# GpSimd subtracts the mean from tiles 4 to 7 in the layer norms over 1024 features

## The chip, the cores and the metric

The kernel runs on one core of a Trainium2 chip. The core has TensorE (PE in the profile), VectorE (DVE), ScalarE (ACT), GpSimd (POOL) and a sync engine (SP) that issues DMAs. Time is device microseconds (us) of one execution.

## The reference, cut to what matters

Two model blocks run one after the other on 512 positions of 1024 features, in float32. The first block has six layer norms over the 1024 features, three in each of its two layers:

```python
def layer_norm(x, g, b):
    mu = jnp.mean(xf, axis=-1, keepdims=True)
    var = jnp.mean(jnp.square(xf - mu), axis=-1, keepdims=True)
    y = (xf - mu) * lax.rsqrt(var + LN_EPS) * g + b
...
for l in range(DEPTH):                       # DEPTH is 2
    ...                                      # a mixer gives y
    x = layer_norm(ALPHA * x + y, ln_mix_g[l], ln_mix_b[l])
    y = memory_cross_attention(x, mem_n, ...)
    x = layer_norm(ALPHA * x + y, ln_xa_g[l], ln_xa_b[l])
    y = swiglu_ffn(x, ffn_wg[l], ffn_wu[l], ffn_wd[l])
    x = layer_norm(ALPHA * x + y, ln_ffn_g[l], ln_ffn_b[l])
```

Two more layer norms (of the memory, and of 512 convolution channels) and the RMS norms of the second block are computed by the same engines and are not changed.

## The kernel before, in words

**Layout.** The activations `xs` lie in on-chip memory as 8 tiles (k = 0 to 7) of 128 features by 512 positions. Each float32 product is made of three matmuls: every operand is split in a high part (`xh`, `w_hi`) and the rest (`xl`, `w_lo`), and `mm3` (L630) adds high by high, high by rest and rest by high. ScalarE makes the high parts, VectorE the rests. Weights come in 205 units of 128x2048, double buffered: SP loads `w_raw`, ScalarE copies it to `w_hi` (`split_hi`, L1139), VectorE subtracts to get `w_lo` (`split_lo`, L1627), and TensorE may begin a unit only when its `w_lo` is there.

**Order.** There is no scheduler. Each engine has its own hand-written list, and the engines meet at semaphores. An engine that waits holds all that stands behind it in its list.

**A layer norm.** The names are mixn0, xan0, ffnn0, mixn1, xan1, ffnn1 in order of time. TensorE sums `xs` and its squares over the features by matmuls with ones, so each sum is already broadcast to all 128 partitions. ScalarE copies the mean out of the bank (L1170, it signals `mean_ready`) and squares it into `rstd` (L1171). Then VectorE runs `normalise` (L1704):

1. `centre(0)`: subtract the mean from tile 0 (L1710);
2. `variance`: mean of squares minus squared mean (L1689, one input a bank, one on chip), then clamp and add epsilon (L1691). ScalarE takes Ln and Exp of it (L1161, L1163) and signals `rstd_ready`;
3. `centre(1)` to `centre(3)`;
4. in the four norms with a filler (mixn0, xan0, ffnn0, mixn1), `w_lo` of a filler unit;
5. for k = 0 to 7: multiply tile k by `rstd` (L1724), then `centre(k + 4)` while k + 4 is below 8, then `then(k - 1)`. With a filler, `w_lo` of one more unit stands in front of k = 2;
6. `then(7)` and `w_lo` of the next unit.

`then(k)` makes the rest `xl` of tile k (L1635), after ScalarE has applied gain and bias to the tile (L1198) and made its high part `xh` (L1152). In ffnn0 `then` is `pool`, the causal window means of the next mixer (L2118, L2110, L2124), which run on VectorE for a pair of tiles at every odd k. In ffnn1 it also collects sums of squares, and ScalarE makes a square for each tile too (L1158).

**Fillers.** In the four norms with a filler, TensorE computes two units of keys or values of the memory while the statistics are made. In xan1 and ffnn1 there is nothing to put there, and TensorE waits for tile 0.

**GpSimd** only clears a few tiles and issues DMAs: constants at the start, then, at L606 to L610, it waits until TensorE has used the unit ahead of glr (near 1421 us), clears part of `wgk` and loads `wgk` and two constants for the second block.

Of the kernel before, what the change touches and what calls it, by code (L numbers as in the profile page):

```python
# [25 lines left out]
ALU = mybir.AluOpType  # L26
# [4 lines left out]
KT = D // P  # L31
# [88 lines left out]
def plan_banks():  # L120
# [24 lines left out]
    def pairs(stage, n):  # L145
        for j in range(n):
            pair(stage, j)

    def norm(name, has_mean=True):
        if has_mean:  # L150
            fill((name, "mean"), 6)
        fill((name, "sq"), 7)
# [15 lines left out]
    def linear_attention(name, filler):  # L168
        for h in range(HEADS):
            fill((name, "scores", h), 4)  # L170
            fill((name, "kend", h), 5)
            if filler:
                pair(*filler[2 * h])
            if h:
                fill((name, "ssq", h - 1), 6 + h % 2)
            fill((name, "o", h, 0), 6 + h % 2)
            fill((name, "ds", h, 0), 4)
            fill((name, "ds", h, 1), 5)
            if filler:
                pair(*filler[2 * h + 1])  # L180
            fill((name, "ds", h, 2), 4)
            fill((name, "ds", h, 3), 5)
        fill((name, "ssq", HEADS - 1), 6)
# [62 lines left out]
    pairs("g", 2), pairs("a1", 1), pairs("q", 2), pairs("v", 2)  # L246
    linear_attention("hg", HG_FILLER)
    norm("cvn")
# [44 lines left out]

FILLER = {"mixn0": "mk1a", "xan0": "mk1b", "ffnn0": "mv1a", "mixn1": "mv1b"}
SUMMED = 2
HG_FILLER = [("mk0", j) for j in range(4)] + [("mv0", j) for j in range(4)]
SWA_ITEMS = 16
plan_banks()
# [30 lines left out]
class Seen:  # L329
# [18 lines left out]
    "sq_ready",  # L348
    "sq_used",
    "mean_ready",  # L350
    "var_ready",
    "rstd_ready",
    "zn_ready",
# [21 lines left out]
def build(nc, x, mem, params, consts, table, w_gk2, sinks, w, out):  # L375
    scratch = nc.dram_tensor("rel_scratch", [16, 384], F32, kind="Internal").ap()
    with ExitStack() as ctx:
        def sb(stack, name, shape, dt=F32):
            return stack.enter_context(nc.sbuf_tensor(name, shape, dt))

        def new_sem(name):
            return ctx.enter_context(nc.semaphore(name))

        sem = {n: new_sem(n) for n in SIGNALS}
# [40 lines left out]
        xs = sb(ctx, "xs", [P, KT, T])  # L425
# [8 lines left out]
        mean = sb(ctx, "mean", [P, T])  # L434
# [79 lines left out]
        def bank(key):  # L514
            return banks[FILL[key][0]]
# [9 lines left out]
        def wait_free(eng, key, i=None):  # L525

            b, n, per = FILL[key][:3]
            if n:
                eng.wait_ge(bank_free[b], at(i, per, n))

        def wait_drained(eng, key, i=None):

            b, n, per = FILL[key][:3]
            eng.wait_ge(bank_free[b], at(i, per, n + 1))
# [4 lines left out]
        def col(name, k=0):  # L539
            c = COL[name] + k  # L540
            return prm[:, c:c + 1]
# [40 lines left out]
        @block.gpsimd  # L582
        def _(pool):
            def const(dst, name, signal, rows=P):
                c = CCOL[name]
                pool.dma_start(dst, consts[0:rows, c:c + dict(CONSTS)[name]]).then_inc(signal, 16)


            pool.memset(ones[:, :], 1.0).then_inc(ones_ready, 1)
            pool.wait_ge(ones_ready, 1)  # L590
            pool.memset(cu[:, :, 0:TAPS - 1], 0.0).then_inc(ones_ready, 1)
            pool.dma_start(prm[:, :], params).then_inc(prm_loaded, 16)
            pool.wait_ge(x_loaded[3], 16)
            pool.dma_start(mk[:, :, :], mem).then_inc(mem_loaded, 16)
            const(sum_q[:, :], "scan32", scan32_loaded)
            const(hmask[:, :], "mask32", hmask_loaded)
            const(ident[:, :], "ident", ident_loaded)
            const(invpos[:, :], "invpos", invpos_loaded)
            pool.dma_start(skb[:, :], sinks.partition_broadcast(P)).then_inc(sinks_loaded, 16)
            pool.wait_ge(ones_ready, 2)  # L600
            pool.memset(tab[32:33, :], NEG).then_inc(ones_ready, 1)
            pool.dma_start(tab[0:32, :], table[0:32, :]).then_inc(table_loaded, 16)

            pool.wait_ge(unit_used, UNITS["glr"])
            pool.wait_ge(ones_ready, 3)
            pool.memset(wgk[96:128, :], 0.0).then_inc(ones_ready, 1)  # L606
            pool.wait_ge(ones_ready, 4)
            pool.dma_start(wgk[112:128, :], w_gk2).then_inc(wgk_loaded, 16)
            const(gmask[:, :], "mask64", gmask_loaded)
            const(scan64[:, :], "scan64", scan64_loaded)  # L610

            pool.wait_ge(unit_used, UNITS["mlp0"])
            const(kk[0:33, 0, 0:384], "onehot", onehot_loaded, 33)
            const(flip[:, :], "flip", flip_loaded)
            wait_drained(pool, ("vec", 0))
            pool.dma_start(scratch, vt[0:16, 0:384]).then_inc(vec_stored, 16)
            pool.wait_ge(vec_stored, 16)

            hankel = bass.AP(tensor=scratch.tensor, offset=0, ap=[[1, P], [384, 16], [1, 2 * P]])
            pool.dma_start(sf[:, :].rearrange("p (h k) -> p h k", h=16), hankel).then_inc(hankel_loaded, 16)  # L620
# [3 lines left out]
        def _(pe):  # L624
            seen = Seen(pe, sem)

            def mm(dst, a, b, start, stop):
                return pe.matmul(dst, a, b, start=start, stop=stop)  # L628
# [51 lines left out]
            def layer_norm_sums(name, x_at, wait_tile, tiles=KT, all_tiles=False):  # L680
# [3 lines left out]
                if all_tiles:  # L684
                    wait_free(pe, mean_)
                    for k in range(tiles - SUMMED):
                        wait_tile(k)
                        mm(bank(mean_)[:, :], ones[:, :], x_at(k), k == 0, False)
                seen.next("sq_used", tiles - SUMMED - 1)
                if not all_tiles:  # L690
# [3 lines left out]
                mm(bank(sq_)[:, :], ones[:, :], sum_q[:, :], True, False)  # L694
                for k in range(tiles - SUMMED, tiles):
                    wait_tile(k)
# [4 lines left out]
            def squares_of_last(key, tiles=KT):  # L701
                seen.skip("sq_ready", tiles - SUMMED)
                for k in range(tiles - SUMMED, tiles):
                    seen.next("sq_ready")
                    last = mm(bank(key)[:, :], ones[:, :], sq[:, k % 2, :], False, k == tiles - 1)
                full(last, key)
# [7 lines left out]
            def rms_norm_sums(name, token_major=False):  # L714

                key, tok = (name, "sq"), (name, "tok")
                seen.next("sq_used", KT - SUMMED - 1)
                wait_free(pe, key)
# [247 lines left out]
            wait_drained(pe, ("v", 1, 1))  # L966
            linear_attention("hg", 32, hq, hk, hs, henb, kend_hg, lambda t, c, n: hv[:, t, c:c + n], 1, HG_FILLER)

# [156 lines left out]
        def _(act):  # L1125
# [309 lines left out]
            def values_out(j):  # L1435
                for m in range(2):
                    key = ("v", j, m)
                    drain(key, hv[:, 2 * m:2 * m + 2, j * 256:(j + 1) * 256], bank(key)[:, :].rearrange("p (t n) -> p t n", t=2))
# [3 lines left out]
            split_hi(UNITS["v"] + 2)  # L1442
            linear_attention("hg", 32, hb, heb, henb, kend_hg, 1.0, 1, lambda h, d: hq[:, h, :], HG_FILLER,
                             lambda: values_out(1))
# [164 lines left out]
        def _(dve):  # L1609
            seen = Seen(dve, sem)  # L1610
            steps = Tally(dve, dve_steps)
# [92 lines left out]
            def normalise(name, n, x_at, tiles, then, unit=None, stage=None):  # L1704


                centred = {}

                def centre(k):
                    centred[k] = steps.step(dve.tensor_tensor(x_at(k), x_at(k), mean[:, :], ALU.subtract))  # L1710

                seen.next("mean_ready")
                centre(0)
                variance(name, n)
                for k in range(1, 4):
                    centre(k)
                if stage:
                    split_lo(unit + 1)
                seen.next("rstd_ready")
                for k in range(tiles):  # L1720
                    if stage and k == 2:
                        split_lo(unit + 2)
                    steps.wait(centred[k])
                    give(dve.tensor_tensor(x_at(k), x_at(k), rstd[:, :], ALU.mult), "zn_ready")  # L1724
                    if k + 4 < tiles:
                        centre(k + 4)
                    if k:
                        then(k - 1)
                then(tiles - 1)
                split_lo(unit + 3 if stage else unit + 1)  # L1730
# [341 lines left out]
            def clear_kpad():  # L2072
# [4 lines left out]
            linear_attention("hg", 32, hq, hk, hb, heb, henb, hmask[:, :], hs, 1, lambda h, d: hq[:, h, :],  # L2077
                             lambda h, d: hg[:, h, :], lambda h, d: col("hg_g", h), HG_FILLER, clear_kpad)
            own("conv_ready")
# [292 lines left out]
```

## Time and profile before

| | |
|---|---|
| median of 3 runs | 2647.96 us (2647.86 to 2650.87) |
| the profiled execution's own time | 2647.57 us |
| its span in the trace | 2645.8 us |
| TensorE busy | 2503.9 us, 95% |
| VectorE busy | 1506.0 us, 57% |
| ScalarE busy | 881.4 us, 33% |
| GpSimd busy | 9.9 us |
| mean granted TensorE clock | 0.976 of 2.4 GHz |

The profiled execution's time is 1.8 us longer than its span and 0.4 us below the median. Busy shares are means over the whole program. In a norm they say little: there TensorE waits and VectorE and ScalarE hand the tiles to each other.

### The profile page before, as it was taken

What the parts mean: (1) busy time and instruction counts of PE and PEld (TensorE: products, weight loads), DVE (VectorE), ACT (ScalarE), POOL (GpSimd) and SP (SyncE); (2) the same over time, 40 slices, a digit from 0 to 9 for tenths busy, and PEclk for the clock granted to TensorE, in tenths of its full rate; (3) what the DMA queues carried; (4) which work ended last, traced back from release to release, by engine and by line L of the source; (5) the groups of instructions that cost most, each with busy time, mean ns of one, the idle gap of its engine ahead of it and who ended that gap; (6) DMA issues with size and microseconds to landing.
All of it is one profiled execution on the core that took longest, in us unless ns stands there. A gap on an engine that the chain in (4) does not pass through costs nothing.

```text
span 2645.8 us, 29702 instructions
## 1 busy us (share of the span) xinstructions
PE 2503.9 (95%) x11776; PEld 2046.3 (77%) x11776; DVE 1506.0 (57%) x2043; ACT 881.4 (33%) x1184; POOL 9.9 (0%) x23
## 2 busy tenths in 40 slices
PE   8998999999999798999997998999999977999998
PEld 7887777788887576888885797788888766788886
DVE  6887544544446835544447436566666467566666
ACT  3434443422223633322224334322222445322222
POOL 0000000000000000000000000000000000000000
PEclk9999999999999899999998999999999998999999
DMA  5222221222222111222221220232222200222221
GB/s 184 80 80 80 80 80 64 96 95 95 95 97 94 64 64 64 93 98 95 95 95 56 93 96 17 92 117 95 95 95 95 80 32 17 84 101 100 96 95 64
DMA packets 32815, 225.56 MB, mean 85 GB/s; under 512 B 3765, under 2 KB 3813, under 8 KB 6368
## 3 DMA queue, kind: packets, MB, share of 16 engines
q1 hardware_dynamic: 31536, 220.21, 24.3%
q0 software_dynamic: 1200, 4.23, 0.4%
q8 instruction: 57, 0.93, 0.1%
q14 instruction: 22, 0.18, 0.0%
HBM read 222.30 MB, written 2.12 MB: 85 GB/s over the span
## 4 chain that ended last, share of the span: by engine, by line
PE 83%; DVE 10%; ACT 5%; issue 1%; DMA 0%; DVEq 0%; SPq 0%; ACTq 0%
PE bank L628 82%; DVE w_lo L1627 2%; ACT w_hi L1139 1%; ACT xs L1198 1%; ACT xh L1152 1%; DVE cacc L1815 1%; DVE xs L1710 1%; DVE xl L1635 0%; DVE mh L2240 0%; DVE xs L1679 0%; DVE rmax L2259 0%; DVE xs L1724 0%; DVE gs L1866 0%; ACT mh L1590 0%; DVE mh L2256 0%
## 5 line engine op out<-in xcount | busy, mean ns | idle before, releaser
L628 PE MATMUL bank<-xh,w_hi 128*128 128x512 f32 x2040 | 816.0, 400 | 62.9 <-DVE xl L1635 27.3
L628 PE MATMUL bank<-xl,w_hi 128*128 128x512 f32 x2040 | 805.7, 395 | 0.0
L628 PE MATMUL bank<-xh,w_lo 128*128 128x512 f32 x2040 | 804.8, 395 | 0.0
L1627 DVE TENSOR_TENSOR w_lo<-w_raw,w_hi 128x2048 fp32r<-128x2048 f32 x205 | 469.7, 2291 | 407.6 <-ACT w_hi L1139 407.1
L1139 ACT ACTIVATE w_hi<-w_raw 128x2048 fp32r<-128x2048 f32 x205 | 391.3, 1909 | 398.6 <-PE bank L628 398.5
L628 PEld LDWEIGHTS bank<-xh,w_hi 128*128 128x128 f32 x2040 | 389.6, 191 | 165.6 <-issue 29.8
L628 PEld LDWEIGHTS bank<-xh,w_lo 128*128 128x128 f32 x2040 | 389.9, 191 | 83.4
L628 PEld LDWEIGHTS bank<-xl,w_hi 128*128 128x128 f32 x2040 | 390.4, 191 | 81.3 <-issue 2.2
L1679 DVE TENSOR_TENSOR xs<-xs,bank 128x512 f32<-128x512 f32 x448 | 294.4, 684 | 116.2 <-PE bank L628 115.1
L628 PE MATMUL bank<-mhh,w_lo 128*128 128x512 f32 x512 | 199.2, 389 | 0.0
L628 PE MATMUL bank<-mhh,w_hi 128*128 128x512 f32 x512 | 199.2, 389 | 0.0
L628 PE MATMUL bank<-mhl,w_hi 128*128 128x512 f32 x512 | 199.2, 389 | 0.0
L1767 DVE TENSOR_TENSOR mh<-bank,rstd 128x512 f32<-128x512 f32 x64 | 43.9, 692 | 178.6 <-PE bank L628 178.6
L1261 ACT ACTIVATE mhh<-mh 128x512 fp32r<-128x512 f32 x64 | 39.5, 633 | 317.3 <-DVE mh L1772 317.3
L628 PE MATMUL bank<-fhh,w_hi 128*128 128x512 f32 x352 | 136.9, 389 | 0.0
L628 PE MATMUL bank<-fhl,w_hi 128*128 128x512 f32 x352 | 136.9, 389 | 0.0
L628 PE MATMUL bank<-fhh,w_lo 128*128 128x512 f32 x352 | 136.9, 389 | 0.0
L1158 ACT ACTIVATE sq<-xs 128x512 f32<-128x512 f32 x88 | 54.6, 630 | 192.1 <-DVE xs L1679 70.7
L628 PEld LDWEIGHTS bank<-mhh,w_lo 128*128 128x128 f32 x512 | 96.1, 188 | 20.1
L628 PEld LDWEIGHTS bank<-mhl,w_hi 128*128 128x128 f32 x512 | 96.1, 188 | 20.0
L628 PEld LDWEIGHTS bank<-mhh,w_hi 128*128 128x128 f32 x512 | 96.1, 188 | 19.9
L1765 DVE TENSOR_TENSOR fh<-sil,bank 128x512 f32<-128x512 f32 x44 | 30.0, 688 | 116.6 <-PE bank L628 109.5
(284 smaller groups left out, 2626.5 us busy)
## 6 DMA issues: line engine op xcount, KB each, us to landing
w_raw<-weights_in SPq DMA_DIRECT2D x205, 1024.0 KB, 5.0
xs<-x_in SPq DMA_DIRECT2D x4, 512.0 KB, 8.1
sf<-rel_scratch POOLq DMA_DIRECT2D x1, 2048.0 KB, 11.8
y_out<-xs SPq DMA_DIRECT2D x8, 256.0 KB, 2.0
w_raw<-weights_in SPq DMA_DIRECT2D x2, 512.0 KB, 6.8
mk<-mem_in POOLq DMA_DIRECT2D x1, 1024.0 KB, 7.2
sum_q<-consts_in POOLq DMA_DIRECT2D x1, 256.0 KB, 7.3
scan<-consts_in POOLq DMA_DIRECT2D x1, 256.0 KB, 2.8
```

Source lines behind the costliest of these rows:

```text
L628: return pe.matmul(dst, a, b, start=start, stop=stop)
L1139: act.activation(w_hi[:, c % 2, :], w_raw[:, c % 2, :], ACT.Copy).then_inc(w_hi_ready, 1)
L1152: give(act.activation((xh if dst is None else dst)[:, k, :], src, ACT.Copy, **kw), "x_hi")
L1158: give(act.activation(sq[:, k % 2, :], src, ACT.Square), "sq_ready")
L1198: give(act.activation(xs[:, k, :], xs[:, k, :], ACT.Identity, scale=col(f"{param}_g{l}", k), bias=col(f"{param}_b{l}", k)), "xn_ready")
L1261: give(act.activation(hh[:, chunk % 2, m, :], src, ACT.Copy), "hh_ready")
L1627: dve.tensor_tensor(w_lo[:, c % 2, :], w_raw[:, c % 2, :], w_hi[:, c % 2, :].bitcast(F32), ALU.subtract)\
L1679: free(dve.tensor_tensor(xs[:, k, :], xs[:, k, :], bank(key)[:, :], ALU.add), key)
L1710: centred[k] = steps.step(dve.tensor_tensor(x_at(k), x_at(k), mean[:, :], ALU.subtract))
L1765: free(dve.tensor_tensor(hid[:, m, :], sil[:, m, :], bank(key)[:, :], ALU.mult), key)
L1767: free(dve.tensor_tensor(hid[:, chunk % 2, m, :], bank(key)[:, :], rstd[:, :], ALU.mult), key)
L1815: ins = dve.scalar_tensor_tensor(a, u, wj, a, ALU.mult, ALU.add)
```

## The change

GpSimd subtracts the mean from tiles 4 to 7 in the six norms over 1024 features: it waits for `mean_ready`, does four subtractions and signals `late_centred` after each. VectorE subtracts it from tiles 0 to 3 only, and waits for `late_centred` ahead of the product with `rstd` of tiles 4 to 7. GpSimd's clear of `wgk` and the DMAs behind it now stand behind all 24 subtractions. The index in `NORMS_WITH_MEAN` plus one is the value of `mean_ready` that belongs to a norm.

```diff
+EARLY = 4
+NORMS_WITH_MEAN = ["memn", "cvn", "mixn0", "xan0", "ffnn0", "mixn1", "xan1", "ffnn1"]
...
+            def centre_late_tiles(norm):
+                pool.wait_ge(sem["mean_ready"], NORMS_WITH_MEAN.index(norm) + 1)
+                for k in range(EARLY, KT):
+                    pool.tensor_tensor(xs[:, k, :], xs[:, k, :], mean[:, :], ALU.subtract).then_inc(sem["late_centred"], 1)
+
+            for norm in NORMS_WITH_MEAN[2:]:
+                centre_late_tiles(norm)
+
             pool.wait_ge(unit_used, UNITS["glr"])
             pool.wait_ge(ones_ready, 3)
+            pool.wait_ge(sem["late_centred"], (KT - EARLY) * len(NORMS_WITH_MEAN[2:]))
             pool.memset(wgk[96:128, :], 0.0).then_inc(ones_ready, 1)
...
-                for k in range(1, 4):
+                for k in range(1, EARLY):
                     centre(k)
...
-                    steps.wait(centred[k])
+                    if k < EARLY:
+                        steps.wait(centred[k])
+                    else:
+                        seen.next("late_centred")
                     give(dve.tensor_tensor(x_at(k), x_at(k), rstd[:, :], ALU.mult), "zn_ready")
-                    if k + 4 < tiles:
-                        centre(k + 4)
```

VectorE's list in mixn0, before, from the clamp of the variance on. `xs<-xs,mean` is a subtraction of the mean, `xs<-xs,rstd` the product with the reciprocal root, `xl` the rest of a tile, `w_lo` the rest of a weight unit:

```order
L1691 TENSOR_SCALAR rstd<-rstd 128x512 [waits bank_free7]
L1710 TENSOR_TENSOR xs<-xs,mean 128x512 x3
L1627 TENSOR_TENSOR w_lo<-w_raw,w_hi 128x2048 [waits w_hi_ready]
L1724 TENSOR_TENSOR xs<-xs,rstd 128x512 [waits dve_steps,rstd_ready]
L1710 TENSOR_TENSOR xs<-xs,mean 128x512
L1724 TENSOR_TENSOR xs<-xs,rstd 128x512 [waits dve_steps]
L1710 TENSOR_TENSOR xs<-xs,mean 128x512
L1635 TENSOR_TENSOR xl<-xs,xh 128x512 [waits x_hi]
L1627 TENSOR_TENSOR w_lo<-w_raw,w_hi 128x2048 [waits w_hi_ready]
L1724 TENSOR_TENSOR xs<-xs,rstd 128x512 [waits dve_steps]
L1710 TENSOR_TENSOR xs<-xs,mean 128x512
```

The same place with the change (its lines are numbered 12 to 15 higher):

```order
L1703 TENSOR_SCALAR rstd<-rstd 128x512 [waits bank_free7]
L1722 TENSOR_TENSOR xs<-xs,mean 128x512 x3
L1639 TENSOR_TENSOR w_lo<-w_raw,w_hi 128x2048 [waits w_hi_ready]
L1739 TENSOR_TENSOR xs<-xs,rstd 128x512 [waits dve_steps,rstd_ready]
L1739 TENSOR_TENSOR xs<-xs,rstd 128x512 [waits dve_steps]
L1647 TENSOR_TENSOR xl<-xs,xh 128x512 [waits x_hi]
L1639 TENSOR_TENSOR w_lo<-w_raw,w_hi 128x2048 [waits w_hi_ready]
L1739 TENSOR_TENSOR xs<-xs,rstd 128x512 [waits dve_steps]
```

Nothing ahead of the first product with `rstd` has moved. Behind it the four single subtractions are gone.

GpSimd's list with the change, from its last DMA of the start to `wgk`; before, the clear of `wgk` followed that DMA directly. The pair of rows that begins with a wait for `mean_ready` comes six times in all, one pair for each norm, and stands once here:

```order
L605 DMA tab<-table_in 32x16
L610 ISA
L610 TENSOR_TENSOR xs<-xs,mean 128x512 [waits mean_ready]
L610 TENSOR_TENSOR xs<-xs,mean 128x512 x3
...
L618 MEMSET wgk 32x512 [waits late_centred,ones_ready,unit_used]
L620 DMA wgk<-w_gk_in 16x512 [waits ones_ready]
```

What moved: 24 subtractions of 128x512 onto GpSimd, and the clear of `wgk` and the DMAs behind the last of them.

## Rows read from the trace of the kernel before

**Rows 1.** The page: engines' busy time, and the shares of the chain that ended last.

```profile
PE 2503.9 (95%) x11776; PEld 2046.3 (77%) x11776; DVE 1506.0 (57%) x2043; ACT 881.4 (33%) x1184; POOL 9.9 (0%) x23
...
PE 83%; DVE 10%; ACT 5%; issue 1%; DMA 0%; DVEq 0%; SPq 0%; ACTq 0%
```

**Rows 2.** L1710 alone: count, ns min/median/max, first and last start.

```profile
L1710 DVE TENSOR_TENSOR xs<-xs,mean x48: 682/685/693, 320.2 to 1438.2; 128x512 f32<-128x512 f32 x48
```

**Rows 3.** Timeline of DVE in mixn0: start us, us, engine, line, what, [idle before, releaser].

```profile
320.15 0.69 DVE L1710 TENSOR_TENSOR xs<-xs,mean 128x512 f32<-128x512 f32 x1 [4.40 <-ACT mean L1170]
320.76 0.68 DVE L1689 SCALAR_TENSOR_TENSOR rstd<-bank,rstd 128x512 f32<-128x512 f32 x1
321.48 0.43 DVE L1691 TENSOR_SCALAR rstd<-rstd 128x512 f32<-128x512 f32 x1
321.82 1.89 DVE L1710 TENSOR_TENSOR xs<-xs,mean 128x512 f32<-128x512 f32 x3
323.63 2.28 DVE L1627 TENSOR_TENSOR w_lo<-w_raw,w_hi 128x2048 fp32r<-128x2048 f32 x1
325.83 0.69 DVE L1724 TENSOR_TENSOR xs<-xs,rstd 128x512 f32<-128x512 f32 x1
...
330.42 2.29 DVE L1627 TENSOR_TENSOR w_lo<-w_raw,w_hi 128x2048 fp32r<-128x2048 f32 x1 [1.49 <-ACT w_hi L1139]
...
333.23 0.68 DVE L1710 TENSOR_TENSOR xs<-xs,mean 128x512 f32<-128x512 f32 x1
...
334.43 0.68 DVE L1724 TENSOR_TENSOR xs<-xs,rstd 128x512 f32<-128x512 f32 x1
...
336.24 0.69 DVE L1724 TENSOR_TENSOR xs<-xs,rstd 128x512 f32<-128x512 f32 x1
```

**Rows 4.** Timeline of ACT in mixn0, tile 0 and tile 3, same columns.

```profile
326.55 0.82 ACT L1198 ACTIVATE xs<-xs,prm 128x512 f32<-128x512 f32 x1 [3.31 <-DVE xs L1724]
...
335.15 0.82 ACT L1198 ACTIVATE xs<-xs,prm 128x512 f32<-128x512 f32 x1 [0.33 <-DVE xs L1724]
```

**Rows 5.** End of mixn0 in the chain that ended last: start us, us, what.

```profile
344.59 0.69 DVE xl L1635
345.28 2.21 DVE w_lo L1627
...
347.54 12.51 PE bank L628 x54
```

**Rows 6.** Timeline of ACT in xan1, tiles 2 and 3.

```profile
1058.88 0.81 ACT L1198 ACTIVATE xs<-xs,prm 128x512 f32<-128x512 f32 x1 [0.17 <-DVE xs L1724]
...
1060.69 0.81 ACT L1198 ACTIVATE xs<-xs,prm 128x512 f32<-128x512 f32 x1 [0.32 <-DVE xs L1724]
```

**Rows 7.** Timeline of DVE in xan1 (first row) and in ffnn0 (the others).

```profile
1052.28 0.69 DVE L1689 SCALAR_TENSOR_TENSOR rstd<-bank,rstd 128x512 f32<-128x512 f32 x1 [0.39 <-PE bank L628]
...
861.44 0.69 DVE L1710 TENSOR_TENSOR xs<-xs,mean 128x512 f32<-128x512 f32 x1
862.23 1.23 DVE L2118 TENSOR_TENSOR pb<-pa 128x1024 f32<-128x1024 f32 x1
```

**Rows 8.** Timeline of POOL: clears of 1 and of 512 columns.

```profile
0.26 0.10 POOL L2362 MEMSET const-float32-0.0<- 128x1 f32 x1 [0.26 <-issue]
...
1421.05 0.52 POOL L606 MEMSET wgk<- 32x512 f32 x1 [1404.19 <-PE bank L628]
```

**Rows 9.** Timeline of DVE beside that last clear.

```profile
1421.14 0.69 DVE L1649 TENSOR_TENSOR sum_q<-sum_q,sq 128x512 f32<-128x512 f32 x1
```

**Rows 10.** Groups of DVE by shape: busy us, mean ns, idle before. One input, on chip or bank.

```profile
L1738 DVE TENSOR_SCALAR xs<-xs 128x512 f32<-128x512 f32 x16 | 5.5, 421 | 0.0
...
L1695 DVE TENSOR_SCALAR rstd<-bank 128x512 f32<-128x512 f32 x13 | 8.9, 687 | 21.7 <-PE bank L628 21.7
```

**Rows 11.** The tile wgk: its first and last matmul start.

```profile
L628 PE MATMUL bank<-mh,wgk x8: 587/587/692, 1483.7 to 1486.8; 32*128 32x512 f32 x8
```

**Rows 12.** Stretches of xan1: busy us by engine, then PEclk, DMA share, GB/s.

```profile
1060.00:1065.00 5.00, 5.00 (x15) 3.90 (x14) 3.67 (x7) 4.61 (x6) 0.00 (x0) 0.58 0.00 0
```

More of the change, by code:

```diff
@@ L350 @@
     "mean_ready",
+    "late_centred",
     "var_ready",
```

## The prediction, made before the changed kernel ran

> **What bounds the kernel now.** I read the page first: TensorE is busy 95% of the span, and 83% of the chain that ended last is TensorE [rows 1]. GpSimd is nearly empty. So a change to VectorE's work counts only where TensorE waits for VectorE, and the six norms are such places. I then read them engine by engine in the timelines. In mixn0 TensorE's next unit starts at 347.54, right behind a `w_lo` that follows the rest of tile 7 at 344.59 [rows 5]. That rest waits for ScalarE, which works through tiles 3 to 7 without a pause for VectorE once tile 3's gain step has begun at 335.15 [rows 4]. So **the second half of a norm goes at ScalarE's pace**, and its end is set by when tile 3's product is there. The first half is VectorE's: from 320.15 to the first product at 325.83 its instructions stand end to end [rows 3], and ScalarE has sat idle for 3.31 us when tile 0 arrives [rows 4]. Whatever delays VectorE in those 5.7 us moves the whole norm. The four subtractions that the change takes from VectorE all stand behind them.
>
> **Part 1: what VectorE loses.** Each subtraction takes 0.685 us by itself [rows 2], but instructions overlap a little: starts lie 0.60 us apart, as 333.23 to the next one shows with two instructions up to 334.43 [rows 3]. Four of them in six norms are 24 x 0.60 = 14.4 us of VectorE. Nearly all of that is off the path, because ScalarE sets the pace. Norm by norm:
> - mixn0, and xan0 and mixn1, whose rows repeat it: tile 3's product starts at 334.43, behind the subtraction at 333.23 [rows 3]. Without it the product is 0.60 us earlier, but ScalarE was idle for only 0.33 us there [rows 4]. Gain 0.3 us each, 0.9 in all. The two subtractions ahead of the `w_lo` at 330.42 give nothing: that one waits for ScalarE, with 1.49 us idle in front of it [rows 3].
> - xan1: ScalarE idles 0.17 and 0.32 us ahead of tiles 2 and 3 [rows 6]. Gain 0.5 us.
> - ffnn0: the subtraction at 861.44 stands directly ahead of the pooling at 862.23 [rows 7], for which everything waits. Gain 0.6 us. The three others there lie in waits.
> - ffnn1: ScalarE has a third step for each tile and is never idle behind tile 0. Gain 0.
>
> Sum: **-2.0 us** (0.9 + 0.5 + 0.6). It is the whole gain that the change can bring.
>
> **Part 2: how long a GpSimd subtraction takes.** No row shows GpSimd reading anything. The nearest are its clears: 0.10 us for one column and 0.52 us for 512 [rows 8], so 0.42 us for one stream of 512 columns. A subtraction has two streams in and one out. If all overlap, it takes 0.52 us, the lower bound. If the three follow one another, it takes 0.10 + 3 x 0.42 = 1.36 us, the upper one. Two inputs in turn with the output beside them would be 0.94. I take 1.15, the middle of the last two, since an engine that needs 0.8 ns for a column that it only writes is unlikely to be as fast when it has to fetch two.
>
> The Trainium skill ("GPSIMD Engine Reference", section 3.1) gives 4497 ns for a float32 `tensor_tensor` of 2048 columns. A quarter of that, 1.12 us, is an estimate from that page, and by it the sum of part 3 would be lower by some 0.7 us. No run here shows it yet.
>
> **Part 3: what these subtractions do to VectorE.** GpSimd is released by the same signal as VectorE's `centre(0)`, so its 4 x 1.15 = 4.6 us fall exactly on the stretch from 320.15 to 325.83. The question is whether both engines can read on-chip tiles at once. The one overlap in the trace is harmless: VectorE's addition at 1421.14 keeps its 0.69 us beside the clear at 1421.05 [rows 8, 9]. But a clear reads nothing. Another pair of rows speaks for a limit on reading: with one on-chip input VectorE needs 0.42 us for 512 columns, and 0.69 when that input is a bank [rows 10]. So it has two ways into on-chip memory and uses both for one tile if it can. A subtraction with two on-chip inputs takes 0.69 us and needs both, and a third reader must share with one of them.
>
> The ends are: no loss (0 us) and full exclusion. For exclusion, I let the engines alternate, each instruction in full:
> - Norms with a filler (four): GpSimd's first subtraction runs behind `centre(0)`, beside the variance step, which takes its second input from a bank; there 0.7 us are free (320.76 to 321.48 [rows 3]). The other three go between the clamp, the three subtractions and the 2.28 us `w_lo`, all ahead of the first product. Delay 4 x 1.15 - 0.7 = 3.9 us each, 15.6 in all.
> - xan1 and ffnn1: VectorE also waits 0.39 us for a bank ahead of the variance [rows 7], so the first subtraction is free. Delay 3 x 1.15 = 3.45 us each, 6.9 in all.
>
> That makes **+22.5 us**. By the bounds of part 2 it would be 4 x 1.38 + 2 x 1.56 = 8.6 (0.52 us a subtraction) or 4 x 4.74 + 2 x 4.08 = 27.1 (1.36 us). A delay of the first product reaches the end of the norm in full. ScalarE waits for it, `w_hi` of the next unit stands behind tile 0 on ScalarE, and the following `w_lo` waits for that. I choose exclusion over no loss because rows 10 are nearer to the case (they are about reading) than rows 9.
>
> What the Trainium skill says on this ("SBUF — State Buffer", section "Who interferes with whom") is sharper: GpSimd's only read port is VectorE's second one, the pair is an exclusive lock for a whole instruction, and a VectorE instruction with two on-chip inputs contends with a GpSimd one that reads. By that rule the sum is the one with exclusion, by rows 9 alone it would be that of part 1. The rule speaks against the change.
>
> **Part 4: the rest.** The wait for tile 4 stands ahead of the product at 336.24, which is 16 us behind the mean [rows 3]. Four GpSimd subtractions need less than 6, so it costs nothing; even in xan1, where tile 4 is due some 10 us after the mean, each could take 2.4 us. With that cover gone, every us of lateness would reach the end. Ahead of its first subtraction GpSimd's list has one instruction of its own kind, `ISA`; it stands in front of the wait, some 300 us early. The clear of `wgk` and three DMAs move from 1421 to behind ffnn1, near 1435, but the first matmul that reads `wgk` starts at 1483.7 [rows 11]: cost 0, with some 45 us to spare. The added wait on `late_centred` at the clear is met by then. PE and ScalarE issue the same lists as before.
>
> **The clock.** When TensorE waits longer, its clock can fall: in xan1 it waited for tile 0, and the stretch behind had a granted clock of 0.58 of 2.4 GHz, so mostly the lower level, 1.2 GHz [rows 12]. There TensorE still kept up with ScalarE. In the norms with a filler the added wait falls between two filler units, where a few us at the lower level would cost 1 to 2 us each. I put 0 in the sum and up to 7 us in the range.
>
> **The sum.** 2647.57 (the profiled execution) + 22.5 - 2.0 = 2668.1. The execution lies 0.4 us below the median of the runs, which is less than what I can resolve. I predict **2668 us**, 0.8% slower.
>
> **Rivals.**
> 1. *Both engines read at once.* It happens ahead of the first product, in all six norms. GpSimd's work is then wholly hidden: 2647.6 - 2.0 = 2645.6, no measurable change. For it: rows 9. Against it: rows 10. It decides on the stretch that one GpSimd subtraction puts on VectorE: below 2.0 / 24 = 0.08 us the kernel gains, and up to 0.3 us each (7.3 / 24) it stays within 0.2%.
> 2. *VectorE goes first.* If VectorE, whose instructions overlap at their ends, holds on to the memory while it has work, GpSimd only gets its turn in VectorE's pauses: beside the variance (1.15 against 0.7 free, +0.45), then in the pause of 1.49 us at 328.9 and in others like it. Price 0.5 to 1.2 us a norm, some +5, less 2.0: near 2650.5. For it: in VectorE's timeline an instruction starts before the one ahead has ended. Against it: a request of GpSimd's that waits is older than VectorE's next one.
> 3. *They share instead of excluding.* Each slows the other in part, say half of part 3: +11 - 2 = 2656.6.
> 4. *The change doesn't do what it says*: an index of `mean_ready` off by one would let GpSimd start in an earlier norm. The sequence memn, cvn, mixn0 and so on agrees with the eight ScalarE copies of a mean, so I give it nothing.
> 5. *A gain above 0.2%* would need 5 us, and part 1 has only 2.0 on the path. It would take a shift of fillers or clock that no row shows.
>
> **How the numbers follow.** Exclusion as summed: 0.50. Sharing in part: 0.12, slower too. VectorE first: 0.13, of which 0.08 within 0.2% and 0.05 above. Both at once: 0.22, within. A gain: 0.03. What a measurement of this kernel can tell from no change is about 0.2%, or 5.3 us, so: faster 0.03, same 0.30, slower 0.67. The range has to reach down to rival 1, since leaving it out would leave out more than 2 in 10: low 2645. At the top stand 1.36 us for a subtraction (+27.1 - 2.0 gives 2672.7) and the clock's 7 us: high 2680. Exclusion's own range is 2654 to 2680.
>
> **What would show it.** Right: in the timeline of mixn0 the stretch from `centre(0)` to the first product grows from 5.7 to about 9.6 us, single VectorE subtractions or the `w_lo` take 1.8 us and 3.4 us instead of 0.69 and 2.28 or start that much later, GpSimd's four start within the first 8 us, ScalarE's idle time ahead of tile 0 grows from 3.3 to some 7 us, and tiles 3 to 7 keep their pace. Part 1 is right if ScalarE no longer idles ahead of tile 3. Wrong: VectorE's instructions there keep 0.69 and 2.28 us and their starts (rival 1); GpSimd's instructions lie in VectorE's pauses (rival 2); VectorE waits for `late_centred` (part 4); or a subtraction takes over 1.4 us (part 2).

## The result and the profile after

The changed kernel takes 2668.01 us in the median of four runs (2666.46 to 2670.38), the kernel before 2649.41 in the same comparison (2647.86 to 2651.97). The ratio is 1.0066, with a 95% interval of 1.0055 to 1.0078: slower by 0.7%. The medians differ by 18.6 us; the profiled execution's span grew from 2645.8 to 2666.4 us, by 20.6. Forecast were 20.5 on top of the profiled execution before (22.5 of price less 2.0 of gain).

The page of the changed kernel, to set beside [rows 1]: VectorE and ScalarE are as busy as before, GpSimd has 38 us more, and the chain has the same shape.

```profile
PE 2508.9 (94%) x11776; PEld 2053.9 (77%) x11776; DVE 1513.7 (57%) x2019; ACT 880.8 (33%) x1184; POOL 47.6 (2%) x47
...
PE 82%; DVE 10%; ACT 5%; issue 2%; DMA 0%; DVEq 0%; SPq 0%; ACTq 0%
```

VectorE lost 24 instructions and still got busier (1513.7 against 1506.0 us). The instructions on the tile `mean` tell why. The columns are those of [rows 2]:

```profile
L1722 DVE TENSOR_TENSOR xs<-xs,mean x24: 677/1750/1797, 320.2 to 1451.9; 128x512 f32<-128x512 f32 x24
L610 POOL TENSOR_TENSOR xs<-xs,mean x24: 1257/1710/1799, 320.3 to 1449.7; 128x512 f32<-128x512 f32 x24
```

A VectorE subtraction took 685 ns at the median, now 1750. GpSimd's take 1257 at the least and 1710 at the median. Both engines show almost the same median, as they would if each had to let one instruction of the other through.

VectorE in mixn0, to set beside [rows 3]:

```profile
320.21 0.69 DVE L1722 TENSOR_TENSOR xs<-xs,mean 128x512 f32<-128x512 f32 x1 [4.40 <-ACT mean L1182]
320.82 0.68 DVE L1701 SCALAR_TENSOR_TENSOR rstd<-bank,rstd 128x512 f32<-128x512 f32 x1
321.53 0.81 DVE L1703 TENSOR_SCALAR rstd<-rstd 128x512 f32<-128x512 f32 x1
322.26 5.16 DVE L1722 TENSOR_TENSOR xs<-xs,mean 128x512 f32<-128x512 f32 x3
327.34 2.28 DVE L1639 TENSOR_TENSOR w_lo<-w_raw,w_hi 128x2048 fp32r<-128x2048 f32 x1
329.54 1.28 DVE L1739 TENSOR_TENSOR xs<-xs,rstd 128x512 f32<-128x512 f32 x2
```

GpSimd beside it:

```profile
320.26 1.79 POOL L610 TENSOR_TENSOR xs<-xs,mean 128x512 f32<-128x512 f32 x1 [303.52 <-ACT mean L1182]
...
320.26 6.61 POOL L610 TENSOR_TENSOR xs<-xs,mean 128x512 f32<-128x512 f32 x4 [303.52 <-ACT mean L1182]
```

The two alternate. The first GpSimd subtraction takes 1.79 us instead of the 1.29 that it needs alone (below), since `centre(0)` began 0.05 us ahead of it; it runs beside the variance step (which keeps its 0.68 us) and pushes the clamp, 0.81 instead of 0.43. The three subtractions of VectorE take 5.16 instead of 1.89 us: (5.16 - 1.89) / 3 = 1.09 us each, one GpSimd subtraction ahead of each. The `w_lo` behind them keeps 2.28 us, since GpSimd is through. The first product starts 3.65 us later, counted from the mean's copy (9.94 against 6.29).

In xan0, xan1 and ffnn1 the order differs: VectorE waits for a bank ahead of the variance, GpSimd's second subtraction meets the clamp, and the last of VectorE's three subtractions is free. The clamp reads one on-chip tile only, yet it loses as much as a subtraction, 1.08 to 1.13 us. In xan0:

```profile
469.27 1.56 DVE L1703 TENSOR_SCALAR rstd<-rstd 128x512 f32<-128x512 f32 x1
```

ScalarE in the same norm, to set beside [rows 4], for tile 0 and tile 3:

```profile
330.26 0.81 ACT L1210 ACTIVATE xs<-xs,prm 128x512 f32<-128x512 f32 x1 [6.59 <-DVE xs L1739]
...
338.43 0.80 ACT L1210 ACTIVATE xs<-xs,prm 128x512 f32<-128x512 f32 x1
```

It idles 6.59 instead of 3.31 us ahead of tile 0, and no longer idles ahead of tile 3. So both the loss and the small gain are there. On TensorE, the longest wait of the stretch 315 to 356 is now the one for the filler's weight rest, 3.7 us in it (before, TensorE waited 0.5 us for a weight rest in this norm):

```profile
PE bank L640 <- DVE w_lo L1639: 4.3, 2, 3.7
PE bank L640 <- DVE xl L1647: 1.7, 1, 1.7
```

**All six norms.** From the start of ScalarE's copy of the mean (L1170, L1182) to two points, in us, read from the timelines. "Product" is the start of the first product with `rstd`, "end" the start of the weight rest behind tile 7 (in ffnn0, the end of the last rest).

| norm | product before | after | end before | after | end, difference |
|---|---|---|---|---|---|
| mixn0 | 6.29 | 9.94 | 25.65 | 28.85 | +3.20 |
| xan0 | 6.80 | 10.14 | 26.15 | 29.05 | +2.90 |
| ffnn0 | 6.36 | 10.06 | 46.07 | 48.96 | +2.89 |
| mixn1 | 6.34 | 9.96 | 25.70 | 28.87 | +3.17 |
| xan1 | 4.59 | 7.82 | 19.63 | 22.24 | +2.61 |
| ffnn1 | 4.60 | 7.81 | 23.24 | 26.45 | +3.21 |
| sum | 34.98 | 55.73 | | | +17.98 |

18.0 of the 20.6 us stand inside the norms, and they begin ahead of the first product (+20.75). The other 2.6 lie between norms: 1.0 behind xan0, 1.4 behind mixn1, 0.2 behind ffnn1. Behind xan0 and mixn1 the kernel before had a granted clock of 1.00 throughout; the changed one has 10 us in each of the two stretches at a mean of 0.83, which is worth at most 0.17 x 10 = 1.7 us each (columns as in [rows 12]):

```profile
845.00:855.00 10.00, 7.21 (x18) 3.59 (x17) 7.34 (x12) 5.54 (x7) 0.00 (x0) 0.83 0.17 45
975.00:985.00 10.00, 7.38 (x31) 6.12 (x30) 6.90 (x15) 2.58 (x9) 0.00 (x0) 0.83 0.33 107
```

That is not the change's doing as far as the runs show. In the three kernels below that leave GpSimd idle, the stretch behind xan0 is longer than before's by 0.95 to 1.15 us too, and the one behind mixn1 by 0 to 1.6 us. So the change is worth some 18 us, and the 18.6 between the medians agree with it.

### The profile page after: what moved, and what is told of

Its sections match the earlier page's. It is cut to its first block, busy times and chain, and to the rows that moved or that the text cites. A ratio compares the mean times of both kernels' runs of the same rounds, so it can differ in the third digit from the quotient of the medians.

```text
span 2666.4 us, 29704 instructions
## 1 busy us (share of the span) xinstructions
PE 2508.9 (94%) x11776; PEld 2053.9 (77%) x11776; DVE 1513.7 (57%) x2019; ACT 880.8 (33%) x1184; POOL 47.6 (2%) x47
## 4 chain that ended last, share of the span: by engine, by line
PE 82%; DVE 10%; ACT 5%; issue 2%; DMA 0%; DVEq 0%; SPq 0%; ACTq 0%
PE bank L640 82%; DVE w_lo L1639 2%; ACT w_hi L1151 1%; ACT xs L1210 1%; ACT xh L1164 1%; DVE xs L1722 1%; DVE cacc L1828 1%; DVE mh L2253 0%; DVE rmax L2272 0%; DVE xs L1691 0%; DVE xl L1647 0%; DVE gs L1879 0%; ACT mh L1602 0%; DVE mh L2269 0%; ACT sq L1170 0%
## 5 line engine op out<-in xcount | busy, mean ns | idle before, releaser
L1170 ACT ACTIVATE sq<-xs 128x512 f32<-128x512 f32 x88 | 54.6, 630 | 192.2 <-DVE xs L1691 70.8
```

Of the source, the lines that this page charges most:

```text
L1170: give(act.activation(sq[:, k % 2, :], src, ACT.Square), "sq_ready")
```

## The experiments

Each kernel was timed against the kernel before on its chip. The chips differ by a few us between runs, so below 0.2% I go by the norm stretches above, one execution of each kernel. Where an edit doesn't reach, they repeat to 0.1 us, save for a step of 0.4 to 0.5 us in the product column that xan0, ffnn0 and mixn1 take in some executions with no edit behind it: VectorE then waits 0.3 to 0.4 us for a bank ahead of the variance, as in [rows 7], and the end of the norm moves with it.

**Is it the reading, or the hand-over?** First, subtractions that nobody uses, with VectorE doing all its old work. Ahead of the products of tiles 4 to 7 VectorE still waits for GpSimd's signal, in this run and in the two that follow, and each GpSimd instruction waits for the one ahead of it:

```diff
+                pool.wait_ge(sem["mean_ready"], i)
+                for k in range(4):
...
+                    pool.tensor_tensor(sum_x[:, :], mean[:, :], mean[:, :], ALU.subtract).then_inc(sem["late_centred"], 1)
...
+                    if k >= 4:
+                        seen.next("late_centred", 4 // 4)
```

> Edit: the kernel before (VectorE subtracts the mean from all eight tiles), and GpSimd beside it does four subtractions of 128x512 in each of the six norms, from the mean's signal on, with a result that nobody uses (mean minus mean, into a tile that is free there). Theory of exclusion: the loss of the change without its gain of 2.0 us, so +22 us against the kernel before (20 to 25), and the stretch from the mean's signal to the first product grows by 3.4 us or more in each norm. Rival, the loss comes from the hand-over of tiles 4 to 7 (VectorE waiting for GpSimd's results) or from the DMAs that moved: then within 3 us of before, since no tile depends on GpSimd.

Measured: 1.0072 (1.0057 to 1.0086), that is +19 us (15 to 23), though no tile takes its values from GpSimd. The norms end 15.5 us later in sum, and the first product 15.6 us, so the delay reaches the end in full. Both are less than expected: the first product comes 2.4 to 2.9 us later in a norm, not 3.4. VectorE's three subtractions in mixn0, and all 24 of GpSimd's:

```profile
319.73 4.42 DVE L1725 TENSOR_TENSOR xs<-xs,mean 128x512 f32<-128x512 f32 x3
```

```profile
L613 POOL TENSOR_TENSOR sum_x<-mean x24: 1038/1367/1546, 318.0 to 1448.8; 128x512 f32<-128x512 f32 x24
```

(4.42 - 1.89) / 3 = 0.84 us for each, less than 1.09: a subtraction that reads one tile twice is shorter (1038 ns at the least) than one of two tiles. The wait for the signal is still there, so the total alone doesn't rule out the hand-over. But VectorE never sits idle for GpSimd, here or in any kernel of this document, and the next run has the same wait.

Then the same with clears, which read nothing:

```diff
+                for k in range(8):
...
+                    pool.memset(sum_x[:, :], 0.0).then_inc(sem["late_centred"], 1)
```

> Edit: as the run with unused subtractions, but GpSimd does eight clears of 128x512 (0.52 us each, so some 4 to 5 us of GpSimd work from the mean's signal on, about as much as four subtractions), which read nothing. Theory of exclusion by reads: 0 to +2 us against before, VectorE's instructions keep 0.69 us. Rival, any GpSimd work beside VectorE (its writes, its power, its signals) costs: +15 to +22 us. The clamp of the variance, one on-chip input in 0.43 us, is the one VectorE instruction that might be touched by writes: at most 0.5 us a norm, 3 us in all.

Measured: 0.9996 (0.9986 to 1.0005); the norms end 2.2 us later in sum. GpSimd works through the same stretch, VectorE waits for the same signal, and its subtractions keep their time. Only the clamp, with one on-chip input and one on-chip output, goes from 0.43 to 0.67 us in mixn0 (0.44 to 0.77 in the others):

```profile
319.19 0.67 DVE L1706 TENSOR_SCALAR rstd<-rstd 128x512 f32<-128x512 f32 x1
319.78 1.88 DVE L1725 TENSOR_TENSOR xs<-xs,mean 128x512 f32<-128x512 f32 x3
```

```profile
317.88 4.78 POOL L613 MEMSET sum_x<- 128x512 f32 x8 [301.00 <-ACT mean L1185]
```

So neither the hand-over nor GpSimd's work as such costs much; its reading does. Nor is it that both engines read the same tile `mean`: the clamp reads only `rstd`, and the weight rest in the late start below reads only weights, and both are pushed. And with one input instead of two (a product of the mean with one):

```diff
-                    pool.tensor_tensor(sum_x[:, :], mean[:, :], mean[:, :], ALU.subtract).then_inc(sem["late_centred"], 1)
+                    pool.tensor_scalar(sum_x[:, :], mean[:, :], 1.0, None, ALU.mult).then_inc(sem["late_centred"], 1)
```

> Edit: as the run with unused subtractions, but GpSimd multiplies the mean by one (one input on chip instead of two). Theory A, any GpSimd instruction that reads on-chip memory excludes VectorE's two-input ones: each of the four delays VectorE by its own length, 0.6 to 0.9 us, less what is free: 1.5 to 2.7 us a norm, +9 to +15 us. Theory B, what hurts is GpSimd's second input: then like the clears, within 3 us of before.

Measured: 1.0029 (1.0020 to 1.0038), +8 us; the norms end 7.6 us later. That is a little under theory A's range and far from theory B's. But theory A was wrong in its mechanism: it had each delay as long as GpSimd's instruction, and that instruction at 0.6 to 0.9 us. Two errors nearly cancel.

```profile
319.86 2.30 DVE L1725 TENSOR_TENSOR xs<-xs,mean 128x512 f32<-128x512 f32 x3
322.08 2.28 DVE L1642 TENSOR_TENSOR w_lo<-w_raw,w_hi 128x2048 fp32r<-128x2048 f32 x1
324.29 1.09 DVE L1741 TENSOR_TENSOR xs<-xs,rstd 128x512 f32<-128x512 f32 x1
```

```profile
L613 POOL TENSOR_SCALAR sum_x<-mean x24: 1491/1540/3137, 318.3 to 1441.9; 128x512 f32<-128x512 f32 x24
```

GpSimd needs 1.54 us at the median, yet a VectorE instruction that meets it loses only 0.41 (2.30 against 1.89, 1.09 against 0.68). So VectorE isn't held up for the whole of the instruction, here for about a quarter of it. Whether GpSimd holds VectorE off for one piece of it or several, no run tells.

**How much is the gain by itself?**

```diff
-                    if k + 4 < tiles:
-                        centre(k + 4)
```

> Edit: nobody subtracts the mean from tiles 4 to 7 in the six norms (that part of the computation is left out); GpSimd stays idle. It measures the gain alone. By part 1 of the prediction: -2.0 us (0.3 in mixn0, xan0, mixn1, 0.5 in xan1, 0.6 in ffnn0, 0 in ffnn1), so 0.999. Rival, VectorE's 14.4 us count in full somewhere: -8 to -14 us.

Measured: 0.9998 (0.9989 to 1.0007), too coarse for 2 us. In the norms the ends come earlier by 0.45, 0.44, 0.37, 0.41, 0.61 and 0.00 us, 2.3 in all. In ffnn0 the first product has the step of 0.43 us here, and without it the end would come 0.8 us earlier, which makes 2.7 in all: the gain of part 1, and far from the 14.4 us of VectorE's work that were taken off. ScalarE starts tile 3 right behind tile 2:

```profile
334.47 0.63 ACT L1152 ACTIVATE xh<-xs 128x512 fp32r<-128x512 f32 x1
335.01 0.80 ACT L1198 ACTIVATE xs<-xs,prm 128x512 f32<-128x512 f32 x1
```

**Does the number of subtractions set the price?** GpSimd takes tile 7 alone, or tiles 6 and 7; VectorE keeps the others in the old order:

```diff
-EARLY = 4
+EARLY = 7
...
-                for k in range(1, EARLY):
+                for k in range(1, 4):
...
+                    if k + 4 < min(tiles, EARLY):
+                        centre(k + 4)
```

> Edit: the change with GpSimd taking tile 7 alone; VectorE subtracts from tiles 0 to 6 in the old order. Theory of exclusion: the single subtraction runs beside the variance step, where only about 0.7 us are free (1.1 us in xan1 and ffnn1), so it delays the first product by 0.4 us or less in each norm and gives nothing back (tile 7's subtraction stood in a pause): 0 to +3 us against before. Rival, a fixed price for each hand-over to GpSimd (start-up, signal, a late tile): +10 us or more already with one tile.

Measured: 1.0007 (0.9998 to 1.0016), norms +1.9 us.

> Edit: the change with GpSimd taking tiles 6 and 7. Theory of exclusion: a second subtraction meets VectorE's busy stretch and adds its whole 1.1 us in each norm, less the gain of tile 6's (2.0 us over all): with one tile plus 6 x 1.1 - 2.0, so +4 to +7 us against before, and the stretch from the mean's signal to the first product grows by 1.1 us from one tile to two. Rival with a fixed price: as with one tile.

Measured: 1.0008 (0.9998 to 1.0017), norms +5.1 us. The two ratios alone don't tell the kernels apart; the timelines do. With one tile only the clamp is pushed in mixn0, with two also one of the three subtractions (2.99 against 1.88):

```profile
319.05 0.80 DVE L1703 TENSOR_SCALAR rstd<-rstd 128x512 f32<-128x512 f32 x1
319.77 1.88 DVE L1722 TENSOR_TENSOR xs<-xs,mean 128x512 f32<-128x512 f32 x3
```

```profile
319.66 0.81 DVE L1703 TENSOR_SCALAR rstd<-rstd 128x512 f32<-128x512 f32 x1
320.39 2.99 DVE L1722 TENSOR_TENSOR xs<-xs,mean 128x512 f32<-128x512 f32 x3
```

The first product starts 1.9 us later in sum with one tile (0.4 of it in mixn0, 0.45 the step in mixn1, and 1.1 in ffnn0, where GpSimd began ahead of `centre(0)`), 7.7 with two, 20.8 with four: the first is nearly free, and from then on each adds some 1.0 to 1.1 us in each norm. There is no fixed price.

**Does it matter where the subtractions lie?**

```diff
                 pool.wait_ge(sem["mean_ready"], NORMS_WITH_MEAN.index(norm) + 1)
+                pool.wait_ge(sem["zn_ready"], 4 + 8 * (NORMS_WITH_MEAN.index(norm) - 2) + 2)
```

> Edit: the change, but GpSimd starts only once VectorE has done the products of tiles 0 and 1 (a wait on the signal of those products). The subtractions then fall on the half that goes at ScalarE's pace, in which VectorE has pauses. Theory of exclusion, with what counts being the stretch ahead of the first product: 0 to +6 us against before, near +3 (in the filler norms the fourth subtraction meets the weight rest by 0.5 us, in xan1 and ffnn1 the two engines have to share a tight half, 1 to 2 us each), so 12 to 18 us less than the changed kernel. Rival, the cost goes with GpSimd's subtractions wherever they lie: +18 to +22 us as in the change.

Measured: 1.0050 (1.0037 to 1.0064), +13 us; the norms end 11.5 us later. **A miss**: better than the change, but four times what I gave it. The first product is on time, save for the step in ffnn0 and mixn1; the ends are 1.1 to 2.1 us late with a filler, 2.8 in xan1 and 2.3 in ffnn1. What I got wrong is how much room the second half has. VectorE in mixn0, the second weight rest and tile 2's product:

```profile
328.13 3.27 DVE L1641 TENSOR_TENSOR w_lo<-w_raw,w_hi 128x2048 fp32r<-128x2048 f32 x1 [1.30 <-ACT w_hi L1153]
331.32 1.77 DVE L1741 TENSOR_TENSOR xs<-xs,rstd 128x512 f32<-128x512 f32 x1
```

```profile
333.13 0.81 ACT L1212 ACTIVATE xs<-xs,prm 128x512 f32<-128x512 f32 x1 [3.66 <-DVE xs L1741]
```

The weight rest loses 0.98 us and the product behind it 1.09, both on the path: ScalarE waits 3.66 us for tile 2, of which 1.60 were there anyway. The path runs through VectorE up to tile 3, not only up to tile 0. GpSimd's first subtraction in ffnn0, with VectorE idle beside it, gives its length by itself:

```profile
857.94 1.29 POOL L612 TENSOR_TENSOR xs<-xs,mean 128x512 f32<-128x512 f32 x1 [379.24 <-DVE xs L1741]
```

**Using the finding without GpSimd.** If the first half is what counts, VectorE's own order should be worth more than the offload:

```diff
-                if stage:
-                    split_lo(unit + 1)
                 seen.next("rstd_ready")
                 for k in range(tiles):
+                    if stage and k == 1:
+                        split_lo(unit + 1)
```

> Edit: the kernel before, GpSimd idle, with one move on VectorE: in the four norms with a filler the product of tile 0 stands ahead of the weight rest of the filler unit (2.2 us) instead of behind it. If the stretch ahead of the first product is what sets the end of a norm, as the theory says, the first product comes 2.2 us earlier and the end of each of the four norms 1.5 to 2.1 us earlier: -6 to -8 us, ratio 0.997, though TensorE gets the second filler unit 0.6 us later. Rival, TensorE's filler sets the pace: the 0.6 us are lost four times, +2.4 us.

Measured: 0.9979 (0.9970 to 0.9988), -5.5 us, a little short of -6 to -8. The norms end 1.58, 1.57, 1.27 and 1.12 us earlier where there is a filler (with the step of 0.4 us in the last two), and not at all in the two others. In mixn0 the first product comes 2.2 us earlier, but less arrives: VectorE has used up its pause of 1.49 us ahead of the second weight rest, so that tile 2's product comes only 1.58 us earlier.

Then the centring of tiles 4 to 7, which the change gave to GpSimd, moved into VectorE's own pauses:

```diff
-                for k in range(1, 4):
+                for k in range(1, 3 if stage else 4):
                     centre(k)
...
-                    if k + 4 < tiles:
-                        centre(k + 4)
+                    if stage and k == 0:
+                        split_lo(unit + 1)
                     if k:
                         then(k - 1)
+                    if stage and k == 1:
+                        centre(3)
+                    for j in {3: (4, 5), 4: (6,), 5: (7,)}.get(k, ()):
+                        if j < tiles:
+                            centre(j)
```

> Edit: the kernel before, GpSimd idle, with VectorE's list in the norms put in the order in which tiles are needed: with a filler, only tiles 0 to 2 are centred ahead of the first product, the filler's weight rest follows that product, tile 3 is centred behind the rest of tile 0, and tiles 4 to 7 are centred from the third product on, in the pauses of the half that goes at ScalarE's pace. The gain that the change was after (four subtractions off the first half) is then had on VectorE itself. By the traces so far: the first product 2.2 to 2.6 us earlier, the second weight rest about 2 to 2.8 us and tile 3 about 2.7 us earlier in each of the four norms with a filler, 0.6 us in xan1, 0 in ffnn1: -9 to -12 us against before, ratio 0.996, some 4 us better than the product moved alone. Rival: the pauses are too short or tile 3 comes late, and it is no better than the product moved alone (0.998).

Measured: 0.9974 (0.9964 to 0.9984), 2640.73 against 2647.78 us: faster than the kernel before and than the changed one. **A miss**: -9 to -12 us were expected, some 4 better than the product moved alone. The two intervals overlap, and the norms end 6.0 us earlier in sum against 5.6 for the product alone, so the rival, that the late centring adds nothing, stands. In mixn0 tile 3's product comes 2.8 us earlier, but the end only 2.06: tile 6 is centred too late, and ScalarE waits for it. In xan1 nothing came of the 0.6 us, and ffnn1 ends 0.2 us later.

```profile
330.36 0.68 DVE L1722 TENSOR_TENSOR xs<-xs,rstd 128x512 f32<-128x512 f32 x1
```

```profile
338.41 0.81 ACT L1198 ACTIVATE xs<-xs,prm 128x512 f32<-128x512 f32 x1 [0.59 <-DVE xs L1722]
```

## Why the prediction was right, point by point

- **What bounds a norm**: right for the change. The delay of the first product (20.75 us in sum) reached the ends, less what part 1 gives back: 17.98. As the prediction put it, "the first half is VectorE's", but the late start showed that VectorE's stretch doesn't close with the first product: up to tile 3 it has little room.
- **Part 1, the gain**: 2.0 us said, 2.7 us measured with the subtractions left out (0.45 instead of 0.3 in mixn0, xan0 and mixn1, 0.6 instead of 0.5 in xan1, 0.8 instead of 0.6 in ffnn0 once the step there is taken off, 0 in ffnn1 as said). The changed kernel agrees: 20.75 - 17.98 = 2.8 us.
- **Part 2, the length**: 1.15 us said; 1.29 alone, inside the bounds of 0.52 and 1.36. The middle was a fair choice, a little low.
- **Part 3, the price**: 3.9 us in a norm with a filler and 3.45 in the other two said, 22.5 in all; 3.3 to 3.7 and 3.2 measured, 20.75. In mixn0 and mixn1 the order was as described: one beside the variance, three ahead of VectorE's three. In the others one of them fell on the clamp or on `centre(0)` instead, at the same price. Each took some 1.1 us from VectorE, close to the 1.15 assumed, but not its own 1.29: the length was put too low, and not the whole of it is lost, and the two nearly cancel. The choice of exclusion by the reading rows [rows 10] over the harmless clear [rows 9] was right, and the clears showed that [rows 9] had said nothing about reads.
- **By the Trainium skill** ("SBUF — State Buffer", section "Who interferes with whom") a VectorE instruction with two on-chip inputs contends with a GpSimd one that reads, and not with one that only writes: the trace agrees, with 1.09 and 0.84 us for the subtractions and 0 for the clears. The same page (section "SBUF: two separate sides") has the loser blocked for the whole of the other's instruction. There the measurement decides otherwise: 1.09 us lost to an instruction of 1.29, and 0.41 to one of 1.54.
- **Part 4, the rest**: right. VectorE never waited for `late_centred`, the `ISA` ahead of the first subtraction cost nothing, and `wgk` was cleared at 1451.56, 52 us ahead of its first matmul:

```profile
1451.56 0.52 POOL L618 MEMSET wgk<- 32x512 f32 x1 [0.15 <-POOL xs L610]
```

```profile
L640 PE MATMUL bank<-mh,wgk x8: 587/587/692, 1504.1 to 1507.2; 32*128 32x512 f32 x8
```

- **The clock**: 0 in the sum, up to 7 us in the range. What is left outside the norms is 2.6 us, and no run ties it to the change.
- **Luck**: that the forecast hit to 0.1 us. The norms cost 18.0 us, 2.5 less than said: the price was put 1.75 us too high and the gain 0.8 too low. What made up for most of it is the base, 2647.57 us, which lay 1.8 us below the median of the kernel before in the same comparison.
- **The rivals**: both at once is out, by the subtractions of 1750 ns. Sharing at half the price is out by the 20.75 us, though the one-input instruction shows a loss of only 0.41 of 1.54 us. VectorE first is out: in the changed kernel the engines take turns, and in ffnn0 GpSimd even came first (VectorE's `centre(0)` there takes 1.80 us).

## What to carry to other kernels

An idle engine is not a free one: before work goes to GpSimd, look at what VectorE does at that moment, and count each GpSimd instruction that reads as a pause of VectorE, unless VectorE reads one of its inputs from a bank. Ask first whether the work that is taken away stood on the path at all (here 2.7 us of 14.4), and where the new one lands (here at the most expensive 6 us of the norm). The cheaper move was to reorder VectorE's own list, product first. Putting the late centring into the pauses as well is not shown to add to it.

## What the runs showed of the hardware

- VectorE and GpSimd took turns, instruction by instruction, when GpSimd read two on-chip tiles and VectorE had two on-chip inputs. VectorE lost 1.09 us to a GpSimd subtraction of two tiles (1.29 us alone), 0.84 to one that reads one tile twice (1.04 at the least) and 0.41 to a one-input product (1.54).
- The clamp of VectorE, one on-chip input in 0.43 us, is pushed as well: it took 1.50 to 1.56 us where it met a whole GpSimd subtraction of two tiles.
- GpSimd's clears (0.52 us) cost VectorE's two-input instructions nothing and its one-input clamp up to 0.34 us.
- A VectorE instruction with one input in a bank kept its 0.68 us beside a GpSimd subtraction.
- It goes both ways: the GpSimd subtractions of the late start that met the 2.28 us weight rest, one in each norm with a filler, took 3.32 to 3.34 us.

```profile
L612 POOL TENSOR_TENSOR xs<-xs,mean x24: 1264/1714/3336, 325.0 to 1449.9; 128x512 f32<-128x512 f32 x24
```
